# Loads ahead of what stood before them in the queue, weighing of values and group sum at other places

## What is computed

```python
h = rms_norm(x, norm_g) * (1 + scale) + shift
q, k, v, z_a, u_b, z_b, g_a, g_b = split(h @ w_in)
for g, (window, dilation) in enumerate(((128, 1), (512, 4), (2048, 16))):
    o[g], lse[g] = dilated attention of q, k, v (4 heads), for prompt and sample tokens
a = sum over g of softmax(lse)[g] * o[g]            # combine_groups
p = pool_mix(u_b)                                   # trailing means over 2, 4, 8, 16 tokens
ya = (a * silu(z_a)) @ w_a_out
yb = (p * silu(z_b)) @ w_b_out
m = sigmoid(g_a) * ya + sigmoid(g_b) * yb
y = x + gate * (m @ w_out)
```

## Time and profile before

| | us |
|---|---|
| median of 3 runs | 2184.86 (2183.28 to 2186.05) |
| the profiled execution | 2182.39 |
| its span in the profile | 2180.6 |
| TensorE busy | 2079.2 (95%) |
| VectorE busy | 1090.7 (50%) |
| ScalarE busy | 689.0 (32%) |
| GpSimd busy | 338.7 (16%) |

### The profile page before, as it was taken

How to read it: one execution, slowest core, us unless ns; L and a number is a source line. 1 busy time by engine, 2 the same in 40 slices (tenths; PEclk the granted TensorE clock), 3 DMA queues, 4 the chain that set the end, 5 groups by cost and what they waited for, 6 DMA issues and landing times.

```text
span 2180.6 us, 38700 instructions
## 1 busy us (share of the span) xinstructions
PE 2079.2 (95%) x13575; PEld 1977.1 (91%) x13575; DVE 1090.7 (50%) x2691; ACT 689.0 (32%) x2278; POOL 338.7 (16%) x453
## 2 busy tenths in 40 slices
PE   5999999999999999999999999899969987999999
PEld 3889999999999999999999999899958976998887
DVE  3543333334434444343422455487757757666664
ACT  4633333333333333333361111333333332111010
POOL 2222112112111111121105565000000000000000
PEclk9999999999999999999999999999989999999999
DMA  9756675664555646554336653678955564544432
GB/s 348 246 178 198 206 223 191 202 203 152 185 171 174 197 144 198 169 166 146 93 97 202 192 202 129 207 192 204 265 164 155 144 198 159 187 153 144 145 128 61
DMA packets 292924, 387.96 MB, mean 178 GB/s; under 512 B 26212, under 2 KB 251828, under 8 KB 291341
## 3 DMA queue, kind: packets, MB, share of 16 engines
q1 hardware_dynamic: 237945, 343.48, 49.9%
q10 hardware_dynamic: 54812, 42.33, 6.8%
HBM read 277.54 MB, written 196.40 MB: 217 GB/s over the span
## 4 chain that ended last, share of the span: by engine, by line
PE 85%; DVE 5%; DMA 3%; SPq 2%; issue 2%; ACT 2%; POOL 1%; ACTq 0%; DVEq 0%
PE a_pp L1081 12%; PE a_pp L1079 12%; PE a_pp L1080 12%; PE g_bank L1079 4%; PE g_bank L1081 4%; PE g_bank L1080 4%; PE pp L1079 3%; PE pp L1081 3%; PE pp L1080 3%; PE c_py L1079 3%; PE c_py L1081 3%; PE c_pa L1080 3%; PE c_pa L1081 3%; PE c_py L1080 3%; PE c_pa L1079 3%
## 5 line engine op out<-in xcount | busy, mean ns | idle before, releaser
L1079 PE MATMUL a_pp<-a_wH,hH 128*128 128x384 f32 x1520 | 527.2, 347 | 5.8 <-DVE qkv L1721 5.2
L1081 PE MATMUL a_pp<-a_wH,hL 128*128 128x384 f32 x1520 | 514.8, 339 | 0.0
L1080 PE MATMUL a_pp<-a_wL,hH 128*128 128x384 f32 x1520 | 513.0, 338 | 0.0
L1710 DVE TENSOR_SCALAR a_ms<-a_ss 128x2 f32<-128x2 f32 (+1 forms) x204 | 34.4, 169 | 520.9 <-ACT a_junk L1599 520.8
L1079 PEld LDWEIGHTS a_pp<-a_wH,hH 128*128 128x128 f32 x1520 | 286.0, 188 | 9.7 <-ACT qkv L1605 4.4
L1079 PE MATMUL g_bank<-hH,aH 128*128 128x258 f32 x896 | 260.4, 291 | 27.8 <-DVE hL L665 21.4
L1080 PEld LDWEIGHTS a_pp<-a_wL,hH 128*128 128x128 f32 x1520 | 286.3, 188 | 0.0
L1081 PEld LDWEIGHTS a_pp<-a_wH,hL 128*128 128x128 f32 x1520 | 285.3, 188 | 0.0
L1599 ACT ACTIVATE a_junk<-a_pp 128x128 f32<-128x128 f32 x384 | 106.6, 278 | 540.9 <-PE a_pp L1081 534.7
L1507 POOL TENSOR_TENSOR a_rs<-a_ms,a_mhalf 128x2 f32<-128x2 f32 (+1 forms) x204 | 140.9, 691 | 838.2 <-DVE a_ms L1710 838.2
L1081 PE MATMUL g_bank<-hH,aL 128*128 128x258 f32 x896 | 257.7, 288 | 0.0
(11 more groups left out here) (290 smaller groups left out, 3939.5 us busy)
## 6 DMA issues: line engine op xcount, KB each, us to landing
out_dram<-in_state_kv_w_dram SPq DMA_DIRECT2D x64, 1023.5 KB, 5.6
qkv_dram<-qkv SPq DMA_DIRECT2D x192, 192.0 KB, 2.1
qkv_in<-qkv_dram SPq DMA_DIRECT2D x192, 192.0 KB, 2.6
a_wst<-in_w_in_dram SPq DMA_DIRECT2D x38, 512.0 KB, 7.2
gl<-gT_dram SPq DMA_DIRECT2D x64, 264.0 KB, 3.9
gT_dram<-out ACTq DMA_DIRECT2D x64, 257.0 KB, 6.2
w<-in_w_in_dram SPq DMA_DIRECT2D x64, 256.0 KB, 6.4
out_dram<-in_state_kv_w_dram SPq DMA_DIRECT2D x8, 2044.0 KB, 11.2
```

What stands on the lines that cost most here:

```text
L1079: nc.tensor.matmul(out, sH, mH, start=(i == 0), stop=False)
L1080: nc.tensor.matmul(out, sH, mL, start=False, stop=False)
L1081: last = nc.tensor.matmul(out, sL, mH, start=False, stop=(i == len(terms) - 1))
L1710: nc.vector.tensor_scalar(ms[0:rows, s % 2, :], ss[0:rows, s % 2, :], 1.0 / E, EPS, ALU.mult, ALU.add).then_inc(meaned, 1)
```

## The change

- `gate_weights` can load some of its four blocks. The blocks for step 1 are issued right behind the token region of product 5 and ahead of the keys and queries of sample 0. Those for step 9 are issued within step 7: three ahead of token region 4, one ahead of region 6.
- The shifted copy of sample 7 goes from step 7 to step 10. Weight piece 0 of the combine stage is issued in step 9 instead of step 8. The values of samples 2 and 3 are issued one step apart.
- VectorE splits token region 5 in step 0 at i = 1, ahead of the weight sums, instead of at i = 2 behind them.
- `weigh` on VectorE goes from i = 2 to i = 3, TensorE's `values` from i = 5 to i = 6 (steps 9 to 12).
- The inputs of the first combine chunk (`zl`, `bl` and the first four `gl`) are issued in step 14 instead of step 15, and no longer wait for the last weight part. For this `gl` and `abL` lie at other places in memory.
- `sum_groups` is cut in two: the maximum and difference (`group_diff`) for both halves and both exps at i = 2 of step 14, the rest (`group_rest`) for half 0 at i = 3 of step 14, for half 1 at i = 0 of step 15. It was half 0 at i = 0 and half 1 at i = 5 of step 14.
- The high part of the pooling branch is made at i = 1 instead of 2 of step 15; weight piece 3 is split within step 15, and the later pieces' places in `LATE_HI` and `LATE_LO` are others.

```diff
--- before.py
+++ after.py
@@ -387,10 +387,11 @@
...
 
-                def gate_weights(s):
+                def gate_weights(s, blocks=range(4)):
 
                     f = s % GP
-                    for i, (c0, kh) in enumerate(((CGA, K1), (CGA, K2), (CGB, K1), (CGB, K2))):
+                    for i in blocks:
+                        c0, kh = ((CGA, K1), (CGA, K2), (CGB, K1), (CGB, K2))[i]
                         if s:
@@ -439,6 +440,7 @@
...
                 install(0, 5)
+                gate_weights(1)
                 keys(0)
@@ -450,12 +452,12 @@
...
                     for s in range(GS):
-                        if s + 1 < GS:
+                        if s + 1 < GS and s not in (0, GP):
                             gate_weights(s + 1)
...
                             keys(s + 1)
-                        if s < NS:
-                            shifted_copy(sp, v, 0, s, bulk)
+                        if s < NS - 1 or s == GP + 2:
+                            shifted_copy(sp, v, 0, min(s, NS - 1), bulk)
                         if s == 2:
@@ -464,38 +466,41 @@
...
                             for i in range(1, NP):
+                                if i == 4:
+                                    gate_weights(GP + 1, range(3))
+                                if i == 6:
+                                    gate_weights(GP + 1, (3,))
                                 sp.wait_ge(g_done, NP * s + i)
...
                                 values(b)
-                            sp.wait_ge(g_done, NP * GP)
-                            load_weights(0)
                             sp.wait_ge(p_ready, 2)
...
                             sp.dma_start(pn[:, :], pnew_dram.rearrange("b h g -> b (h g)")).then_inc(pn_moved, 16)
-                        if GP + 2 <= s < GP + 5:
-                            for b in range(2):
-                                values(2 * (s - GP - 1) + b)
+                        if s == GP + 1:
+                            sp.wait_ge(g_done, NP * GP)
+                            load_weights(0)
+                        for b in {GP + 1: (2,), GP + 2: (3,), GP + 3: (4, 5), GP + 4: (6, 7)}.get(s, ()):
+                            values(b)
                         if s == GP + 5:
...
                                 sp.dma_start(ol[i][:, :, :], o_dram[i * P:(i + 1) * P, :, :]).then_inc(ol_landed[i], 16)
-                        if s == GS - 1:
+                        if s == GS - 2:
                             for i in range(2):
                                 sp.wait_ge(b_stored[i], 16 * PAIRS * NBC // 2)
-                            sp.wait_ge(g_lo, NP * GS)
                             branch_inputs(0)
+                            for i in range(4):
+                                sp.wait_ge(g_stored[i], 16 * GP)
+                            gates(0, range(4))
+                        if s == GS - 1:
                             for n, freed in enumerate((0, 2, 4, 5, 1, 3, 6), 1):
...
                                 load_weights(n)
-                                if n == 2:
-                                    for i in range(4):
-                                        sp.wait_ge(g_stored[i], 16 * GP)
-                                    gates(0, range(4))
                     for i in range(4):
@@ -725,12 +730,12 @@
...
                                                         AX.X, ALU.add).then_inc(snew_ready, 1)
+                            if s == 0 and i == 1:
+                                token_lo(0, 5)
                             if i == 1 and s + 1 < GS:
...
                                 weight_lo(s + 1, n)
-                            if s == 0 and i == 2:
-                                token_lo(0, 5)
                             if s == GP - 1 and i == 3:
@@ -755,10 +760,10 @@
...
                                 dve.wait_ge(pT_ready, 1)
-                            if s == GP + 1 and i == 2:
+                            if s == GP + 1 and i == 3:
                                 weigh(0)
-                            if GP + 2 <= s < GP + 5 and i in (0, 2):
-                                weigh(2 * (s - GP - 2) + i // 2 + 1)
+                            if GP + 2 <= s < GP + 5 and i in (0, 3):
+                                weigh(2 * (s - GP - 2) + i // 3 + 1)
                             if s == GP + 5 and i == 0:
@@ -783,10 +788,16 @@
...
                                 dve.wait_ge(aTs_ready, 1)
-                            if s == GS - 2 and i in (0, 5):
-                                n = i // 5
-                                dve.wait_ge(ol_landed[n], 16)
-                                sum_groups(nc, ol[n][:, :, :], cw[:, n], chained, ol_diff, lambda: dve.wait_ge(ol_exp, n + 1)).then_inc(a_ready, 1)
+                            if s == GS - 2 and i == 2:
+                                for n in range(2):
+                                    dve.wait_ge(ol_landed[n], 16)
+                                    group_diff(nc, ol[n][:, :, :], cw[:, n], chained, ol_diff)
+                            if s == GS - 2 and i == 3:
+                                dve.wait_ge(ol_exp, 1)
+                                group_rest(nc, ol[0][:, :, :], cw[:, 0], chained).then_inc(a_ready, 1)
+                            if s == GS - 1 and i == 0:
+                                dve.wait_ge(ol_exp, 2)
+                                group_rest(nc, ol[1][:, :, :], cw[:, 1], chained).then_inc(a_ready, 1)
                             if s == GS - 1:
@@ -799,8 +810,8 @@
...
                                     attention_lo()
-                                if i == 5:
-                                    weights_lo(2)
+                                if i >= 5:
+                                    weights_lo(i - 3)
                     for i in range(4):
@@ -906,16 +917,19 @@
...
                                 nc.scalar.activation(a_odd, psA[QUAD:QUAD + NS, :], ACT.Copy).then_inc(odd_read, 1)
-                            if s == GS - 2 and i in (0, 5):
-                                group_exp(i // 5)
+                            if s == GS - 2 and i == 2:
+                                for n in range(2):
+                                    group_exp(n)
                             if s == GS - 1:
-                                if i == 2:
+                                if i == 1:
                                     pooling_hi()
...
                                     weights_hi(2)
+                                if i == 6:
+                                    weights_hi(3)
                 m["scalar"](act, stage)
@@ -1027,10 +1041,10 @@
...
                                 last.then_inc(turned, 1)
-                            if s == GP + 1 and i == 5:
+                            if s == GP + 1 and i == 6:
                                 values(0)
-                            if GP + 2 <= s < GP + 5 and i in (3, 5):
-                                values(2 * (s - GP - 2) + (i - 3) // 2 + 1)
+                            if GP + 2 <= s < GP + 5 and i in (3, 6):
+                                values(2 * (s - GP - 2) + (i - 3) // 3 + 1)
                             if s == GP + 5 and i == 3:
@@ -1047,14 +1061,28 @@
...
 
-    m, l = o[:, :, E + 1:E + 2].rearrange("p n o -> p (n o)"), o[:, :, E:E + 1].rearrange("p n o -> p (n o)")
+    group_diff(nc, o, cw, chained, diff_ready)
+    wait_exp()
+    return group_rest(nc, o, cw, chained)
+
+
+def group_diff(nc, o, cw, chained, diff_ready):
+
+    m = o[:, :, E + 1:E + 2].rearrange("p n o -> p (n o)")
+    by_head = m.rearrange("p (g h) -> p h g", h=HEADS)
+    as_groups = lambda ap: ap.rearrange("p (g h) -> p g h", h=HEADS)
+    chained(nc.vector.tensor_reduce(cw[:, 0, 0:HEADS], by_head, AX.X, ALU.max))
+    nc.vector.tensor_tensor(as_groups(cw[:, 1, :]), as_groups(m), cw[:, 0, 0:HEADS].unsqueeze(1).to_broadcast([P, GROUPS, HEADS]),
+                            ALU.subtract).then_inc(diff_ready, 1)
+
+
+def group_rest(nc, o, cw, chained):
+
+    l = o[:, :, E:E + 1].rearrange("p n o -> p (n o)")
     by_head = lambda ap: ap.rearrange("p (g h) -> p h g", h=HEADS)
...
     row = lambda k: cw[:, k, :]
-    chained(nc.vector.tensor_reduce(row(0)[:, 0:HEADS], by_head(m), AX.X, ALU.max))
-    nc.vector.tensor_tensor(as_groups(row(1)), as_groups(m), over(row(0)[:, 0:HEADS]), ALU.subtract).then_inc(diff_ready, 1)
-    wait_exp()
     chained(nc.vector.tensor_tensor(row(3), row(2), l, ALU.mult))
@@ -2027,14 +2055,15 @@
...
         abH = sb("abH", [P, KT, CS], F32R)
-        abL = sb("abL", [P, KT, CS], F32R)
-        gl = [sb(f"gl{i}", [P, 2, CS]) for i in range(RG)]
         bl = sb("bl", [P, 4, CS])
         zl = sb("zl", [P, 4, CW])
+        sb("pad1", [P, 32])
+        gl = [sb(f"gl{i}", [P, 2, CS]) for i in range(RG)]
+        abL = sb("abL", [P, KT, CS], F32R)
         a32 = sb("a32", [P, 4, CS])
...
         m_s = sb("m_s", [P, KT, NS])
-        sb("pad2", [P, 120])
+        sb("pad2", [P, 88])
```

(2 more changed lines are left out.)

## The result

| us | before | after |
|---|---|---|
| median of 5 runs each | 2186.05 (2183.28 to 2186.77) | 2172.97 (2167.25 to 2175.13) |
| ratio, 95% interval | | 0.9938 (0.9924 to 0.9953) |
| the profiled execution | 2182.39 | 2172.97 |
| its span | 2180.6 | 2170.9 |
| TensorE busy | 2079.2 (95%) | 2087.0 (96%) |

A forecast was written before the change was run, and what follows sets the result against it. TensorE, 95% busy, was taken as the bound, with only its gaps and the slow matmuls behind them to win. Terms 4.6+7.9+2.9+11.1 = 26.5 off 2182.39 gave 2155.9, plus 2.5 for the median 2158.4; range 2152 to 2168.

The forecast's parts named there:

- A: Step 0: weights loaded and token part made earlier shorten the gap before product 5; 4.6 us saved, bounds 2.5 and 6.5.
- C: Steps 9 and 10: weigh and values() one product later shorten TensorE's gaps; 2.9 us saved, bounds 1 and 4.5.
- B: Steps 7 and 8: earlier weights for step 9 let product 5 of step 8 start 7.9 us sooner, bounds 4 and 9.5.
- D: Steps 14 and 15 into the combine stage: earlier inputs, split group sum, moved weight pieces; 11.1 us saved, bounds 6 and 13.
- The 1.91 gap: TensorE's gap ahead of product 0 of step 8: claimed to stay, as nothing ahead of it moves.
- rivals 2 and 4: 2: split sum and new step 15 gap cost more, 2163.5, chance 0.12; 4: slower, clock low around short gaps, 2190, 0.02.
- rival 1: Queue in steps 0 and 8: tokens and queries land later than 3.3 us per MB says; 2165.4, chance 0.12.

The follow-up runs named there:

- e2: The kernel before with part A alone: 2185.26 us, ratio 0.9998.
- e6: The changed kernel with the values of sample 2 issued behind the weights of step 11 again: 2166.51 us, ratio 0.9909.
- e1: The changed kernel with part A undone: 2168.82 us, ratio 0.9915.
- e3: The kernel before with part B alone: 2179.9 us, ratio 0.9969.
- e4: The kernel before with part C alone: 2186.3 us, ratio 0.9997.
- e5: The kernel before with part D alone: 2175.66 us, ratio 0.9943.
- e7: The changed kernel with the shifted copies of samples 0 to 6 moved from steps 0 to 6 to steps 8 and 10 to 12: 2160.37 us, ratio 0.988.
- e9: The changed kernel with both the copies moved as in e7 and the order of values and weights as in e6: 2156.39 us, ratio 0.9869.
- e11: The kernel e9 with part C undone: 2157.72 us, ratio 0.9875.
- e10: The kernel e9 without part A: 2160.86 us, ratio 0.9888.
- e8: The kernel before with the shifted copies of samples 0 to 6 moved as in e7: 2179.25 us, ratio 0.9964.

## Why the prediction was wrong

The forecast was 2158.4 us with 2152 to 2168 as its range; the time is 2172.97. The step that failed first is the sum: it adds A's 4.6 us whole and has no term for steps 1 to 7, so it takes it that a lead won in step 0 passes through them unharmed. The second is in C, where the new place of values(2) in SyncE's queue "costs nothing". In the traces 0.1 is left of A's 4.6, steps 3 to 7 lose 5.6 (forecast 0), B gives 9.4 (7.9), 0.7 is lost behind it, steps 9 and 10 lose 3.6 (forecast a gain of 2.9) and D gives 11.2 (11.1). By the medians of the parts alone A gives 0.8, B 6.2, C -0.2 and D 9.9.

**A: the gain in step 0 was right, that it lasts was wrong.** In step 0 all came as worked out: the query lands at 1408.40 (forecast 1407.6, and this trace starts the stage 0.4 later), the gap is 1.68 + 3.63 = 5.3 us in two parts (forecast 5), product 6 starts 4.6 us earlier. What follows in the next two steps on VectorE:

```profile
1408.40 0.69 DVE L628 TENSOR_TENSOR prod<-kt,qb 128x512 f32<-128x512 f32 x1 [7.83 <-DMA qb<-samp_dram]
...
1411.65 2.29 DVE L670 TENSOR_TENSOR hL<-m_raw,hH 128x2056 fp32r<-128x2056 f32 x1
...
1436.98 0.69 DVE L704 TENSOR_TENSOR w<-w 128x512 f32<-128x512 f32 x1 [4.41 <-DMA w<-in_w_in_dram]
```

The last weight block of step 2 is issued at 1425.39 in after and at 1427.53 in before, so it does move up. But from issue to landing it takes (the last number, before first):

```profile
w<-in_w_in_dram SPq DMA_DIRECT2D x1, 256.0 KB, 5.5
w<-in_w_in_dram SPq DMA_DIRECT2D x1, 256.0 KB, 11.6
```

So it lands at 1436.95 instead of 1433.02, 3.9 us later. This is no chance of one execution: the same block takes 11.5 to 11.7 us in after, e2 and e6, which have A and the copies, 5.5 to 6.1 in before, e1, e3, e4 and e5, which lack A, and 6.6 to 7.0 in e7, e9 and e11, which have A and no copies in steps 0 to 6. It takes both, A and the copy ahead of it in the queue. ScalarE's stores of the gate outputs also take longer (in after a median of 10.1 us against 6.6 in before, between 1418 and 1440 us). Why the block pays so much stays open. Had it landed as in before (36.4 us from the start of the stage), VectorE would have waited some 0.9 us for it and not 4.41, by my estimate from these rows: so here it wasn't the length of the circuit that ate the lead, but a load that was twice as long on its way.

Two gaps (1.27 and 2.69 us, each 0.16 more from start to start) and 0.2 us of slower matmuls give back 4.5 us. The prediction asked what is late next in step 0 only. It had written for the earlier trace rows that full stretches can't be made shorter and from that took it that a lead passes through them unharmed. A stretch is only as good as its slack, and this one had 1 us in step 5. With the circuit shortened, A is worth 4.5 (e9 against e10).

**Steps 3 to 7: no term at all.** From 2,1 to 7,6 they lost 5.6 us in after and in e2 and 6.0 in e5, but 1.2 in e3 and nothing in e6. The change has no edit there, and e5 has no edit ahead of them. It is the circuit with the landing times of an execution, and with the copies out of the way (e7, e8, e9, e10, e11) nothing is lost there. Which transfer makes a block late in one execution and not in another stays open, and so does what spreads the times: after's runs lie 7.9 us apart, those of e9 2.6, but those of e7, without the copies too, 10.1.

**B: the mechanism was right, the size in part luck.** Forecast 7.9; measured from 7,6 to 8,5 9.4 in after, 8.9 in e6, 9.2 in e7, but 6.1 in e3, alone, where the median gives 6.2. VectorE in step 8, where it waited 8.08 us for weights before:

```profile
1592.15 0.69 DVE L704 TENSOR_TENSOR w<-w 128x512 f32<-128x512 f32 x1 [0.61 <-DMA w<-in_w_in_dram]
...
1596.81 2.29 DVE L670 TENSOR_TENSOR hL<-m_raw,hH 128x2056 fp32r<-128x2056 f32 x1
```

The gap is 4.51 us, a bit under the 5 to 7 forecast. In part the gain in after may be larger than the term because the long gap of before also absorbs what steps 1 to 7 lost: e2, e4 and e5, without B, win 1.3 to 2.9 here. The 1.91 gap that was to stay is 0.62 in after, with one of 2.18 ahead of it in step 7.

**C: wrong in sign.** Step 9 gave 1.6 us in after (9,0 to 10,0; forecast 1.9), in the two gaps that were forecast (2.53 and 1.98 us, forecast about 2.3 each). Step 10 should have given 1.0 and took 5.2. The step that failed is the sentence on SyncE's queue: the last weight block can't go before weight part 5, "some 2 us later" than the wait for values(), so the wait costs nothing, and VectorE's slack of 3 us covers it if it does. Part 5 came 1.5 us behind the end of values() (1633.20), but SyncE had then still three loads of values and three blocks to issue, so the last block went 2.0 us late. It also landed late: it took 10.0 to 10.6 us in the four kernels with this order (after, e1, e4, e7) and 5.7 to 7.6 in all others. VectorE waited 3.36 us. Of these its slack covered 2.4 for product 5, whose gap is the 0.94 at 1653.83. But weigh(2) stands behind the same weight sums, and for it there was no slack at all: its gap was there in before (the 1.95 of the earlier trace rows), so each us that VectorE is late goes into it, and it became 3.29 with 2.0 of slow matmuls behind. I had costed the delay against the one consumer that had room. With the wait gone C wins 1.3 us or nothing (e11 less e9): in step 9 VectorE waits 6.6 us for weights ahead of all this (at 1610.67 in e9), and both gaps come behind that landing, so the order of VectorE's work changes little.

**D: right, 11.2 for 11.1** (alone 9.9 by the medians and 12.4 in its trace, so the match to 0.1 is luck). The new gap ahead of step 15 is 2.62 us (forecast 3.1), ended by the sum L692 behind the first group sum; VectorE's gate multiplication starts without a wait where it waited 5.06 us; column 4 waits 4.04 (forecast 5), the output 0.47 for 2.23. VectorE's timeline, steps 14 and 15 of after:

```profile
1756.13 1.76 DVE L1090 TENSOR_TENSOR ol<-ol,cw 128x1536 f32<-128x1536 f32 x1
...
1759.87 0.68 DVE L692 TENSOR_TENSOR sums<-g_bank,sums 128x516 f32<-128x516 f32 x1
...
1769.44 0.69 DVE L2276 TENSOR_TENSOR a<-c_pT,zl 128x512 f32<-128x512 f32 x1
```

**The clock** was a small part of it. Summed over TensorE's rows from 1396 to 1850 us, idle gaps, counted from start to start, fell by 15.1 us (59.5 to 44.4), and the time that matmuls behind them took above their distance at 2.4 GHz rose by 4.6 (16.6 to 21.2); 10.5 together, near the 10.8 of the table. So rivals 2 and 4 name something real and small, and the circuit that decided was among none of the four.

**The queue's price** of 3.32 us for a transfer of 1028 KB held (rival 1 did not happen): the query landed within 0.4 us of where it puts it, counted from the start of the stage. By the 6.15 us that the Trainium skill, page "DMA: Bandwidth & Descriptors", section "Measured", has for 1 MB moved alone from GpSimd, it would by estimate have landed 2.8 us later than that.

## What to carry to other kernels

A full stretch of the bound engine can hide a second circuit (load, prepare, free the buffer, load again) of nearly the same length. Ahead of counting a lead through such a stretch, add up one turn of it from the other engines' waits, and compare it with the bound engine's step: where less than the lead is left, the lead is lost. And look at when each load lands and not at when it is issued: a block issued 2.1 us sooner landed 3.9 us later here. Bulk transfers without a date belong where no load with a date stands behind them; and of an issue that is moved behind a new wait, count all that stands behind it in that queue, to the last block.

## What I had not expected of the hardware

- A 256 KB weight block, the same instruction in the same place, took 9.3, 9.5 and 10.7 us from its issue in three consecutive steps of one execution (the chain of after above). At 1425.39 it took 11.56 us, and 11.5 to 11.7 in each of the three traces with part A and the copies.
- Whether slow matmuls follow a gap of about 2 us was not set by its length: behind 1.98 us at 1631.76 they cost 1.2 us, behind 2.69 us at 1449.35 0.1, both in after; behind 1.91 us in before 1.6, behind 1.95 nothing.
